# A residual block stack on one Trainium2 core: the modulation's scaling and sums moved between the two pairs of units of a feed-forward quad

## The chip, the cores and the metric

One core of one Trainium2 chip runs the whole program. The metric is device time of one execution in microseconds (us); the median of three runs is given.

## The reference

A first block of two layers works on 16 meta tokens and 256 tokens of width 1024: a feed-forward, a mixer (a short convolution, then differential attention), a second feed-forward, each with an RMS norm before and behind it. That makes four feed-forwards, numbered 0 to 3 here. A second block of two layers follows, whose norms are scaled, shifted and gated by a modulation computed from a vector c:

```
def swiglu(h, w_gu, w_down):
    g, u = jnp.split(h @ w_gu, 2, axis=-1)
    return (jax.nn.silu(g) * u) @ w_down
...
cond = jax.nn.silu(c)
for l in range(DEPTH):
    mod = cond @ ada_w[l] + ada_b[l]
    shift, scale, gate = jnp.split(mod, 3, axis=-1)
    h = rms_norm_2(x, norm_g[l]) * (1.0 + scale[:, None, :]) + shift[:, None, :]
```

The hidden width of a feed-forward is 2816, and `ada_w` has 1024 x 3072 numbers for each of two layers. The modulation depends on c alone, so it can be computed at any time before the second block.

## The kernel before

**Units and quads.** All large weights come in units of 128 output columns, four units a quad, one for each of four slots of the buffers `raw`, `w_hi` and `w_lo`. A unit (i, s) goes through: SyncE loads `raw` slot s (L543); ScalarE rounds it to `w_hi` (`split_hi`, L591) once the slot's earlier unit is through on TensorE; VectorE makes `w_lo = raw - w_hi` (`split_lo`, L1069); TensorE multiplies three times for each of 8 chunks of 128 rows (L1773 to L1775), since each operand is split in an upper and a lower half.

**A feed-forward** (`ffn(k)`, stages `gu{k}` and `dn{k}`) has two halves. The first has 11 quads (0 to 10). The units of a quad are gate, up, gate, up: two pairs p = 0, 1, each giving one of 22 hidden chunks. Per pair VectorE scales the gate's bank (`tg`, L1167) and the up's bank (`ur`, L1170), multiplies (`full`, L1175) behind ScalarE's SiLU (`silu`, L679), ScalarE rounds the product to `a_hi` (`hi`, L683), VectorE subtracts to `a_lo` (`lo`, L1181). In quad i both engines also split the units of quad i+1. The second half, the down projection, has 4 quads of wider units (1408 columns of a slot, 33 matmuls); units 0 and 1 of a quad fill bank 0 with hidden chunks 0 to 10 and 11 to 21, units 2 and 3 bank 2. Feed-forwards 0 to 2 work on 272 tokens, feed-forward 3 on 256.

**The modulation** is computed in the shadow: 12 pieces per feed-forward (`ada_w`, 512 KB each). SyncE loads a piece into the one buffer `ada_raw` (L554), ScalarE scales its eight parts by `cond` (`am`, L667), VectorE adds them up in three steps (`a0`, `a1`, `ar`; L1157, L1160, L1163).

**What orders the work.** Each engine runs its instructions in the order written. An engine counts its steps on a semaphore of its own, in the order that `vec.phase` and `act.phase` declare (L297, L298), and others wait for a count. SyncE's queue repeats: the four weight loads of quad i (slot s waits for `w_lo` of unit (i-1, s)), then the modulation piece i, which waits for `ar` of quad i-1:

```
def load_ada(k, i):
...
    sp.wait_ge(vec.sem, gu_step(vec, f"gu{k}", "ar", i - 1))
...
with sp.Fori(2 if stage[:2] == "gu" else 1, n) as i:
    load(stage, i)
    if stage[:2] == "gu":
        load_ada(k, i)
```

The functions that the diff touches, with what calls them:

Of the kernel before, what the change touches and what calls it, by code (L numbers as in the profile page):

```python
# [117 lines left out]
def build(nc, w8, w11, ada_w, params_in, consts_in, masks_in, pool_w, bands_in, fl_w, x_in, out):  # L118
    ctx = ExitStack()
    with ctx:  # L120
# [110 lines left out]
        act, vec, pe, pool = (Steps(sem(n)) for n in ("scalar_steps", "vector_steps", "tensor_steps", "gpsimd_steps"))  # L231
# [56 lines left out]
        def declare_ffn(k):  # L288
            g, d = f"gu{k}", f"dn{k}"
            if k == 0:  # L290
                act.phase("pre0", [f"hi{c}" for c in range(DC)] + [f"sq{c}" for c in range(DC)])
                vec.phase("pre0", [f"lo{c}" for c in range(DC)])
            act.phase(g + "q", ["am"])
            declare_stat(f"pre{k}")
            act.phase(g + "r", ["silu0", "silu1", "hi0", "hi1"])
            vec.phase(g + "q", ["a0", "a1", "ar", "tg0", "ur0", "tg1", "ur1", "full0", "lo0", "full1", "lo1"])
            act.phase(g, ["am", "silu0", "hi0", "silu1", "hi1"], 10)  # L297
            vec.phase(g, ["tg0", "a0", "a1", "ar", "ur0", "full0", "lo0", "tg1", "ur1", "full1", "lo1"], 10)  # L298
            act.phase(d + "a", ["am"])
            act.phase(d, ["sq0", "f0", "sq1", "f1"], 4)  # L300
            pool.phase(d, ["zero"])
            pool.phase(d + "s", ["add0", "add1"], 3)
            pool.phase(d + "t", ["add0"])
            vec.phase(d, ["a0", "a1", "ar"])
            declare_res(f"res{k}")
            pe.phase(d, ["ada"])
# [276 lines left out]
        def _(sc):  # L583
# [79 lines left out]
            def ada(phase, i):  # L663

                sc.wait_ge(ada_in, 16 * i + 16)
                for c in range(DC):
                    last = sc.activation(ada_raw[:, c, :], ada_raw[:, c, :], ACT.Copy, scale=cond[:, c:c + 1])  # L667
                last.then_inc(act.step(phase, "am"), 1)

            def ffn(k):  # L670
                g, d = f"gu{k}", f"dn{k}"
                n = width(g)
                ada(g + "q", 12 * k)
                token_norm(f"pre{k}")
                sc.preload_act_table(ACT.Silu)

                def silu(phase, p, i):
                    sc.wait_ge(vec.sem, gu_step(vec, g, f"tg{p}", i))
                    sc.activation(silu_t[:, p, 0:n], xt[:, p, 0:n], ACT.Silu).then_inc(act.step(phase, f"silu{p}"), 1)  # L679

                def upper_a(phase, p, i):
                    sc.wait_ge(vec.sem, gu_step(vec, g, f"full{p}", i))
                    sc.activation(a_hi[:, bass.ds(2 * i + p, 1), 0:n].rearrange("p a t -> p (a t)"), u_t[:, p, 0:n], ACT.Copy  # L683
                                  ).then_inc(act.step(phase, f"hi{p}"), 1)

                for p in range(2):
                    silu(g + "r", p, 0)
                for p in range(2):
                    upper_a(g + "r", p, 0)

                def gu_quad(i):
                    ada(g, 12 * k + i)
                    for p in range(2):
                        split_next(g, i, 2 * p)
                        silu(g, p, i)
                        split_next(g, i, 2 * p + 1)
                        upper_a(g, p, i)

                gu_quad(1)
                with sc.Fori(2, 10) as i:  # L700
                    gu_quad(i)
                gu_quad(10)

                sc.preload_act_table_set("natural_log_exp_and_others")
                ada(d + "a", 12 * k + 11)
                first = GAIN[f"res{k}"][1]

                def dn_quad(i):
                    q = FIRST_QUAD[d] + i
                    for p in range(2):  # L710
                        o = 2 * i + p
                        split_next(d, i, 2 * p)
                        sc.wait_ge(unit_done, SLOTS * q + 2 * p + 2)
                        if not isinstance(i, int) or i > 0:
                            sc.wait_ge(pool.sem, pool.at(d + "s", f"add{p}", i - 1))
                        sc.activation(sq[:, p, 0:n], bank[2 * p][:, 0:n], ACT.Square).then_inc(act.step(d, f"sq{p}"), 1)  # L716
                        sc.activation(f[:, bass.ds(o, 1), 0:n].rearrange("p a t -> p (a t)"), bank[2 * p][:, 0:n],
                                      ACT.Copy, scale=half_g[:, first, bass.ds(o, 1)]).then_inc(act.step(d, f"f{p}"), 1)
                        if not (isinstance(i, int) and i == 3 and p == 1):
                            split_next(d, i, 2 * p + 1)  # L720

                quads(d, dn_quad)
                res_norm(f"res{k}")
# [339 lines left out]
        def _(ve):  # L1063
# [86 lines left out]
            def ffn(k):  # L1150
# [27 lines left out]
                def lower_a(phase, p, i):  # L1178
                    at = bass.ds(2 * i + p, 1)
                    ve.wait_ge(act.sem, gu_step(act, g, f"hi{p}", i))  # L1180
                    ve.tensor_tensor(a_lo[:, at, 0:n].rearrange("p a t -> p (a t)"), u_t[:, p, 0:n],  # L1181
                                     a_hi[:, at, 0:n].rearrange("p a t -> p (a t)").bitcast(F32), ALU.subtract
                                     ).then_inc(vec.step(phase, f"lo{p}"), 1)
# [14 lines left out]
                def gu_quad(i):  # L1198
                    q = FIRST_QUAD[g] + i
                    for p in range(2):  # L1200
                        ve.wait_ge(unit_done, SLOTS * q + 2 * p + 1)
                        gate(g, p, bank[2 * p])
                        split_next(g, i, 2 * p)
                        if p == 0:
                            ada(g, i, i - 1, act.at(g, "am", i - 1))
                        ve.wait_ge(unit_done, SLOTS * q + 2 * p + 2)
                        ve.wait_ge(vec.sem, gu_step(vec, g, f"lo{p}", i - 1))
                        up(g, p, bank[2 * p + 1])
                        full(g, p, i)
                        split_next(g, i, 2 * p + 1)  # L1210
                        lower_a(g, p, i)

                gu_quad(1)
                with ve.Fori(2, 10) as i:
# [554 lines left out]
        def _(te):  # L1769
# [119 lines left out]
            def ada(k, units):  # L1889

                for i in units:
                    last = te.matmul(ADA[:, i:i + 1], ada_sum[:, i, :], ones[:, 0:1], start=True, stop=True)
                return last
# [11 lines left out]
            def ffn(k):  # L1905
                g, d = f"gu{k}", f"dn{k}"
                n = width(g)
                free = lambda s, i: (vec.sem, gu_step(vec, g, ("tg", "ur")[s % 2] + str(s // 2), i))
                second_quad(f"pre{k}", g, n, free(3, 0))
                later_quads(g, n, free)  # L1910

                def dn_quad(i):
                    q = FIRST_QUAD[d] + i
                    for s in range(SLOTS):
                        te.wait_ge(w_lo_ready, SLOTS * q + s + 1)
                        p = s // 2
                        if isinstance(i, int) and i == 0:
                            if s == 0:
                                te.wait_ge(vec.sem, vec.at(g, "lo0", 9))
                            if s == 1:  # L1920
                                te.wait_ge(vec.sem, vec.at(g, "lo1", 9))
                        elif s % 2 == 0:
                            te.wait_ge(act.sem, act.at(d, f"f{p}", i - 1))
                        if isinstance(i, int) and i == 3 and s == 3:
                            res_most(f"res{k}", pool.at(d + "t", "add0"))
                        for kk in range(HALF):
                            kc = HALF * (s % 2) + kk
                            last = product(bank[2 * p][:, 0:n], s, kk, a_hi[:, kc, 0:n], a_lo[:, kc, 0:n],
                                           kc == 0, kc == FC - 1)
                        last.then_inc(unit_done, 1)  # L1930
                dn_quad(0)
                with te.Fori(1, 3) as i:
                    dn_quad(i)
                dn_quad(3)
                te.wait_ge(vec.sem, vec.at(d, "ar"))
                ada(k, range(2))
                res_last(f"res{k}", act.at(d, "sq1", 3))
                ada(k, range(2, 12)).then_inc(pe.step(d, "ada"), 1)
# [576 lines left out]
```

## Time and profile before

| | |
|---|---|
| median of 3 runs | 1402.84 us (1402.38 to 1402.99) |
| profiled execution | 1399.22 us, its span 1397.4 us |
| TensorE busy | 1334.0 us (95%) |
| VectorE busy | 920.1 us (66%) |
| ScalarE busy | 806.8 us (58%) |
| GpSimd busy | 81.0 us (6%) |
| DMA | 239.99 MB, mean 172 GB/s |

Times in the trace are from the start of the span. A row of a timeline gives an instruction's start, its length, engine, line and operands, and in brackets how long the engine stood idle before it and what ended that. PE is TensorE, DVE VectorE, ACT ScalarE, SP SyncE. Lengths of pipelined instructions overlap a little with the next; what an instruction takes of its engine is the distance between two starts.

### The profile page before, as it was taken

The page shows a single profiled execution, that of the slowest core. Times are in us where ns is not written, and L with a number is a line of the kernel's source. Part 1 is how long each engine was busy: PE and PEld are TensorE (multiplying, and loading weights), DVE is VectorE, ACT ScalarE, POOL GpSimd, SP SyncE. Part 2 cuts the span into 40 slices and gives each one's busy share as a digit, 9 for nine tenths or more (in the row PEclk, how much of TensorE's full clock was granted, in tenths as well). Part 3 has the DMA queues.
Part 4 walks back from the last instruction along what each step waited for, and adds up shares of the span by engine and source line. Part 5 has one row for each costly group of instructions (what it writes and reads, how often), then busy time and mean ns, then how long its engine had stood idle before and what let it go on. Part 6 is the DMA issues. An engine that isn't in the chain of part 4 may idle for free.

```text
span 1397.4 us, 27554 instructions
## 1 busy us (share of the span) xinstructions
PE 1334.0 (95%) x10214; PEld 1288.2 (92%) x10214; DVE 920.1 (66%) x1525; ACT 806.8 (58%) x1570; POOL 81.0 (6%) x81
## 2 busy tenths in 40 slices
PE   6999999998999999999999999899999899989997
PEld 6999999998999999999998988799999899977787
DVE  5777536866777536777536776577764574666774
ACT  6666544446666546666535555676664543457663
POOL 2000011012000001000001000300000000010000
PEclk9999999999999999999999999999999999999999
DMA  5766653653766652766643441466675254445441
GB/s 192 248 225 237 228 186 123 187 166 107 247 224 240 227 168 87 246 228 236 225 140 109 128 122 48 136 227 226 225 248 163 71 181 121 132 136 147 121 125 35
DMA packets 63314, 239.99 MB, mean 172 GB/s; under 512 B 7024, under 2 KB 8448, under 8 KB 63104
## 3 DMA queue, kind: packets, MB, share of 16 engines
q1 hardware_dynamic: 63168, 238.84, 51.9%
q8 instruction: 56, 0.92, 0.3%
q14 instruction: 26, 0.21, 0.0%
q0 software_dynamic: 64, 0.02, 0.0%
HBM read 237.76 MB, written 1.05 MB: 171 GB/s over the span
## 4 chain that ended last, share of the span: by engine, by line
PE 75%; DVE 10%; ACT 8%; issue 4%; DMA 2%; DVEq 0%; ACTq 0%; POOL 0%; SPq 0%; POOLq 0%
PE bank L1773 20%; PE bank L1775 20%; PE bank L1774 19%; DVE w_lo L1069 4%; PE bank L1780 3%; ACT w_hi L591 2%; ACT ada_raw L667 2%; PE bank L1845 2%; PE bank L1846 1%; PE bank L1838 1%; PE bank L1781 1%; PE bank L2154 1%; DVE ada_raw L1157 1%; DMA ada_raw<-ada_w 1%; DMA raw<-w 1%
## 5 line engine op out<-in xcount | busy, mean ns | idle before, releaser
L1069 DVE TENSOR_TENSOR w_lo<-raw,w_hi 128x1024 fp32r<-128x1024 f32 (+2 forms) x376 | 489.8, 1306 | 321.1 <-ACT w_hi L591 320.6
L1773 PE MATMUL bank<-x_hl,w_hi 128*128 128x272 f32 (+1 forms) x1776 | 516.5, 291 | 15.0 <-DVE w_lo L1069 14.7
L1775 PE MATMUL bank<-x_hl,w_lo 128*128 128x272 f32 (+1 forms) x1776 | 511.0, 288 | 0.0
L1774 PE MATMUL bank<-x_hl,w_hi 128*128 128x272 f32 (+1 forms) x1776 | 509.3, 287 | 0.0
L591 ACT ACTIVATE w_hi<-raw 128x1024 fp32r<-128x1024 f32 (+2 forms) x376 | 411.9, 1101 | 125.7 <-PE bank L1775 107.1
L1773 PEld LDWEIGHTS bank<-x_hl,w_hi 128*128 128x128 f32 x1776 | 335.7, 189 | 18.0 <-ACT arena L627 8.7
L1774 PEld LDWEIGHTS bank<-x_hl,w_hi 128*128 128x128 f32 x1776 | 338.4, 191 | 0.6
L1775 PEld LDWEIGHTS bank<-x_hl,w_lo 128*128 128x128 f32 x1776 | 335.4, 189 | 0.0
L1773 PE MATMUL bank<-a_hi,w_hi 128*128 128x272 f32 (+1 forms) x960 | 279.1, 291 | 11.7 <-DVE w_lo L1069 3.4
L1775 PE MATMUL bank<-a_hi,w_lo 128*128 128x272 f32 (+1 forms) x960 | 275.1, 287 | 0.0
L1774 PE MATMUL bank<-a_lo,w_hi 128*128 128x272 f32 (+1 forms) x960 | 274.6, 286 | 0.0
L1773 PEld LDWEIGHTS bank<-a_hi,w_hi 128*128 128x128 f32 x960 | 182.4, 190 | 14.6 <-DVE w_lo L1069 7.2
L1774 PEld LDWEIGHTS bank<-a_lo,w_hi 128*128 128x128 f32 x960 | 182.7, 190 | 0.4
L1775 PEld LDWEIGHTS bank<-a_hi,w_lo 128*128 128x128 f32 x960 | 182.1, 190 | 0.0
L667 ACT ACTIVATE ada_raw<-ada_raw,cond 128x128 f32<-128x128 f32 x384 | 117.5, 389 | 0.9 <-DMA ada_raw<-ada_w 0.8
L683 ACT ACTIVATE a_hi<-arena 128x272 f32 (+3 forms) x88 | 37.7, 429 | 125.6 <-DVE arena L1175 125.2
L1780 PE MATMUL bank<-x_hl,w_hi 128*128 128x512 f32 x256 | 92.2, 400 | 4.4 <-DVE x_hl L1107 2.8
L1781 PE MATMUL bank<-x_hl,w_lo 128*128 128x256 f32 x256 | 71.7, 280 | 0.0
L1780 PEld LDWEIGHTS bank<-x_hl,w_hi 128*128 128x128 f32 x256 | 48.1, 188 | 16.0 <-issue 5.0
L716 ACT ACTIVATE sq<-bank 128x272 f32<-128x272 f32 (+1 forms) x32 | 12.6, 394 | 85.9 <-PE bank L1775 85.9
L1717 POOL TENSOR_TENSOR sq_sum<-sq_sum,sq 128x272 f32<-128x272 f32 (+1 forms) x28 | 21.4, 764 | 702.3 <-ACT sq L716 702.3
L1845 PE MATMUL bank<-x_hl,w_hi 128*128 128x272 f32 (+1 forms) x144 | 43.0, 321 | 10.4 <-ACT x_hl L623 8.2
(275 smaller groups left out, 1423.1 us busy)
## 6 DMA issues: line engine op xcount, KB each, us to landing
raw<-w SPq DMA_DIRECT2D x312, 512.0 KB, 4.4
raw<-w SPq DMA_DIRECT2D x64, 704.0 KB, 4.6
ada_raw<-ada_w SPq DMA_DIRECT2D x48, 512.0 KB, 3.6
h<-x_in SPq DMA_DIRECT2D x1, 1088.0 KB, 5.3
work<-bands SPq DMA_DIRECT2D x1, 544.0 KB, 7.0
cst<-consts SPq DMA_DIRECT2D x1, 528.0 KB, 4.6
out<-h SPq DMA_DIRECT2D x1, 512.0 KB, 3.0
out<-h SPq DMA_DIRECT2D x4, 128.0 KB, 2.3
```

Of the source, the lines that this page charges most:

```text
L591: sc.activation(w_hi[:, s, a:n], raw[:, s, a:n], ACT.Copy).then_inc(w_hi_ready, 1)
L667: last = sc.activation(ada_raw[:, c, :], ada_raw[:, c, :], ACT.Copy, scale=cond[:, c:c + 1])
L683: sc.activation(a_hi[:, bass.ds(2 * i + p, 1), 0:n].rearrange("p a t -> p (a t)"), u_t[:, p, 0:n], ACT.Copy).then_inc(act.step(phase, f"hi ...
L1069: ve.tensor_tensor(w_lo[:, s, a:n], raw[:, s, a:n], w_hi[:, s, a:n].bitcast(F32), ALU.subtract).then_inc(w_lo_ready, 1)
L1157: ve.tensor_tensor(ada_raw[:, 0:4, :], ada_raw[:, 0:4, :], ada_raw[:, 4:8, :], ALU.add).then_inc(vec.step(phase, "a0"), 1)
L1717: gp.tensor_tensor(sq_sum[:, 0:n], sq_sum[:, 0:n], sq[:, p, 0:n], ALU.add).then_inc(pool.step(phase, f"add{p}"), 1)
L1773: te.matmul(dst, w_hi[:, s, a:a + P], rhs_hi, start=first, stop=False)
L1774: te.matmul(dst, w_hi[:, s, a:a + P], rhs_lo, start=False, stop=False)
L1775: return te.matmul(dst, w_lo[:, s, a:a + P], rhs_hi, start=False, stop=last)
L1780: te.matmul(dst.rearrange("p (a t) -> p a t", a=2), w_hi[:, s, a:a + P], both, start=first, stop=False)
L1781: return te.matmul(dst[:, 0:SEQ], w_lo[:, s, a:a + P], both[:, 0, :], start=False, stop=last)
L1845: te.matmul(dsts[s][:, 0:n], w_hi[:, s, k * P:(k + 1) * P], x_hi[:, k, 0:n], start=k == 0, stop=False)
```

## The change

In quads 1 to 10 of each feed-forward's first half the scaling of a modulation piece (`ada` on ScalarE) stood ahead of the quad's first split, and its sums (`ada` on VectorE) between the first split and `ur0`. Both now stand behind the first pair: behind `hi0` on ScalarE, behind `lo0` on VectorE. The declared orders are changed to match. In the second half, the first unit waited for `lo0` of quad 10; it now waits for `tg0` of quad 10, which is the step that reads bank 0 last; the hidden chunks 0 to 10 that it reads are made in quads 0 to 5.

```diff
--- before.py
+++ after.py
@@ -294,8 +294,8 @@
             declare_stat(f"pre{k}")
             act.phase(g + "r", ["silu0", "silu1", "hi0", "hi1"])
             vec.phase(g + "q", ["a0", "a1", "ar", "tg0", "ur0", "tg1", "ur1", "full0", "lo0", "full1", "lo1"])
-            act.phase(g, ["am", "silu0", "hi0", "silu1", "hi1"], 10)
-            vec.phase(g, ["tg0", "a0", "a1", "ar", "ur0", "full0", "lo0", "tg1", "ur1", "full1", "lo1"], 10)
+            act.phase(g, ["silu0", "hi0", "am", "silu1", "hi1"], 10)
+            vec.phase(g, ["tg0", "ur0", "full0", "lo0", "a0", "a1", "ar", "tg1", "ur1", "full1", "lo1"], 10)
             act.phase(d + "a", ["am"])
             act.phase(d, ["sq0", "f0", "sq1", "f1"], 4)
             pool.phase(d, ["zero"])
@@ -689,12 +689,13 @@
                     upper_a(g + "r", p, 0)
 
                 def gu_quad(i):
-                    ada(g, 12 * k + i)
                     for p in range(2):
                         split_next(g, i, 2 * p)
                         silu(g, p, i)
                         split_next(g, i, 2 * p + 1)
                         upper_a(g, p, i)
+                        if p == 0:
+                            ada(g, 12 * k + i)
 
                 gu_quad(1)
                 with sc.Fori(2, 10) as i:
@@ -1201,14 +1202,14 @@
                         ve.wait_ge(unit_done, SLOTS * q + 2 * p + 1)
                         gate(g, p, bank[2 * p])
                         split_next(g, i, 2 * p)
-                        if p == 0:
-                            ada(g, i, i - 1, act.at(g, "am", i - 1))
                         ve.wait_ge(unit_done, SLOTS * q + 2 * p + 2)
                         ve.wait_ge(vec.sem, gu_step(vec, g, f"lo{p}", i - 1))
                         up(g, p, bank[2 * p + 1])
                         full(g, p, i)
                         split_next(g, i, 2 * p + 1)
                         lower_a(g, p, i)
+                        if p == 0:
+                            ada(g, i, i - 1, act.at(g, "am", i - 1))
 
                 gu_quad(1)
                 with ve.Fori(2, 10) as i:
@@ -1916,7 +1917,7 @@
                         p = s // 2
                         if isinstance(i, int) and i == 0:
                             if s == 0:
-                                te.wait_ge(vec.sem, vec.at(g, "lo0", 9))
+                                te.wait_ge(vec.sem, vec.at(g, "tg0", 9))
                             if s == 1:
                                 te.wait_ge(vec.sem, vec.at(g, "lo1", 9))
                         elif s % 2 == 0:
```

ScalarE, the loop over quads 2 to 9 of feed-forward 0, before (`ada_raw` scaled, `raw_in0` to `raw_in2` the weight slots):

```order
L667 ACTIVATE ada_raw<-ada_raw,cond 128x128 [waits ada_in]
L667 ACTIVATE ada_raw<-ada_raw,cond 128x128 x7
L590 ISA [waits raw_in0]
L591 ACTIVATE w_hi<-raw 128x1024 [waits unit_done]
L679 ACTIVATE silu_t<-xt 128x272 [waits vector_steps]
L590 REGISTER_ALU [waits raw_in1]
L591 ACTIVATE w_hi<-raw 128x1024 [waits unit_done]
L683 ISA [waits vector_steps]
L683 ACTIVATE a_hi<-arena 128x272
L590 REGISTER_ALU [waits raw_in2]
L591 ACTIVATE w_hi<-raw 128x1024 [waits unit_done]
```

and in the changed kernel, where the file's lines behind the edit are one further:

```order
L590 ISA [waits raw_in0]
L591 ACTIVATE w_hi<-raw 128x1024 [waits unit_done]
L679 ACTIVATE silu_t<-xt 128x272 [waits vector_steps]
L590 REGISTER_ALU [waits raw_in1]
L591 ACTIVATE w_hi<-raw 128x1024 [waits unit_done]
L683 ISA [waits vector_steps]
L683 ACTIVATE a_hi<-arena 128x272
L667 ACTIVATE ada_raw<-ada_raw,cond 128x128 [waits ada_in]
L667 ACTIVATE ada_raw<-ada_raw,cond 128x128 x7
L590 REGISTER_ALU [waits raw_in2]
L591 ACTIVATE w_hi<-raw 128x1024 [waits unit_done]
```

The eight scalings have moved from the quad's start to the place between `a_hi` of the first pair and `w_hi` of slot 2.

VectorE, the same loop before (`xt<-bank0` is `tg0`, `arena<-bank1` is `ur0`, `arena<-arena,silu_t` is `full0`, `a_lo` is `lo0`, `xt<-bank2` is `tg1`):

```order
L1167 TENSOR_TENSOR xt<-bank0,arena 128x272 [waits unit_done]
L1069 TENSOR_TENSOR w_lo<-raw,w_hi 128x1024 [waits w_hi_ready]
L1157 TENSOR_TENSOR ada_raw<-ada_raw 128x512 [waits scalar_steps]
L1160 TENSOR_TENSOR ada_raw<-ada_raw 128x256 [waits vector_steps]
L1163 TENSOR_TENSOR arena<-ada_raw 128x128
L1207 ISA [waits unit_done]
L1170 TENSOR_TENSOR arena<-bank1,arena 128x272 [waits vector_steps]
L1175 TENSOR_TENSOR arena<-arena,silu_t 128x272 [waits scalar_steps]
L1069 TENSOR_TENSOR w_lo<-raw,w_hi 128x1024 [waits w_hi_ready]
L1181 TENSOR_TENSOR a_lo<-arena,a_hi 128x272
L1167 TENSOR_TENSOR xt<-bank2,arena 128x272 [waits unit_done]
L1069 TENSOR_TENSOR w_lo<-raw,w_hi 128x1024 [waits w_hi_ready]
```

and in the changed kernel:

```order
L1168 TENSOR_TENSOR xt<-bank0,arena 128x272 [waits unit_done]
L1070 TENSOR_TENSOR w_lo<-raw,w_hi 128x1024 [waits w_hi_ready]
L1171 TENSOR_TENSOR arena<-bank1,arena 128x272 [waits vector_steps]
L1176 TENSOR_TENSOR arena<-arena,silu_t 128x272 [waits scalar_steps]
L1070 TENSOR_TENSOR w_lo<-raw,w_hi 128x1024 [waits w_hi_ready]
L1182 TENSOR_TENSOR a_lo<-arena,a_hi 128x272
L1158 TENSOR_TENSOR ada_raw<-ada_raw 128x512 [waits scalar_steps]
L1161 TENSOR_TENSOR ada_raw<-ada_raw 128x256 [waits vector_steps]
L1164 TENSOR_TENSOR arena<-ada_raw 128x128
L1168 TENSOR_TENSOR xt<-bank2,arena 128x272 [waits unit_done]
L1070 TENSOR_TENSOR w_lo<-raw,w_hi 128x1024 [waits w_hi_ready]
```

The three additions on `ada_raw` and its sum have moved from ahead of the wait for the second unit to behind `a_lo` of the first pair; so has the step `ar`, for which SyncE's next modulation load waits.

## Rows read from the trace of the kernel before

**Rows 1.** The page, part 1: busy us (share) xinstructions.

```profile
PE 1334.0 (95%) x10214; PEld 1288.2 (92%) x10214; DVE 920.1 (66%) x1525; ACT 806.8 (58%) x1570; POOL 81.0 (6%) x81
```

**Rows 2.** Timeline of TensorE, feed-forward 0: start us, us, line, [idle before <-releaser].

```profile
40.10 0.39 PE L1773 MATMUL bank<-x_hl,w_hi 128*128 128x272 f32 x1 [1.12 <-DVE w_lo L1069]
...
43.45 0.39 PE L1773 MATMUL bank<-x_hl,w_hi 128*128 128x272 f32 x1
...
149.01 0.29 PE L1773 MATMUL bank<-a_hi,w_hi 128*128 128x272 f32 x1
```

**Rows 3.** Windows: us, busy of each engine (x), granted clock, DMA share, GB/s.

```profile
52.78:64.26 11.48, 11.48 (x93) 11.48 (x93) 8.96 (x16) 7.77 (x16) 0.00 (x0) 1.00 0.67 230
956.14:967.52 11.38, 11.38 (x99) 11.38 (x98) 8.83 (x16) 7.74 (x16) 0.00 (x0) 1.00 0.65 230
1027.60:1033.50 5.90, 5.86 (x27) 5.89 (x28) 4.39 (x6) 4.97 (x10) 0.00 (x0) 0.50 0.97 369
```

**Rows 4.** Timeline of VectorE, one quad of feed-forward 0.

```profile
84.30 1.23 DVE L1069 TENSOR_TENSOR w_lo<-raw,w_hi 128x1024 fp32r<-128x1024 f32 x1 [2.06 <-ACT w_hi L591]
85.44 0.68 DVE L1157 TENSOR_TENSOR ada_raw<-ada_raw 128x512 f32<-128x512 f32 x1
...
86.75 0.29 DVE L1163 TENSOR_TENSOR arena<-ada_raw 128x128 f32 x1 [0.17 <-DVE ada_raw L1160]
86.97 0.44 DVE L1170 TENSOR_TENSOR arena<-bank,arena 128x272 f32<-128x272 f32 x1
87.54 0.44 DVE L1175 TENSOR_TENSOR arena<-arena,silu_t 128x272 f32<-128x272 f32 x1
87.90 1.22 DVE L1069 TENSOR_TENSOR w_lo<-raw,w_hi 128x1024 fp32r<-128x1024 f32 x1
```

**Rows 5.** Timeline of ScalarE, the same quad.

```profile
80.53 0.43 ACT L683 ACTIVATE a_hi<-arena 128x272 f32 x1 [0.77 <-DVE arena L1175]
80.87 2.45 ACT L667 ACTIVATE ada_raw<-ada_raw,cond 128x128 f32<-128x128 f32 x8
83.22 1.04 ACT L591 ACTIVATE w_hi<-raw 128x1024 fp32r<-128x1024 f32 x1
...
88.12 0.43 ACT L683 ACTIVATE a_hi<-arena 128x272 f32 x1 [2.59 <-DVE arena L1175]
```

**Rows 6.** Timeline of SyncE's queue, that quad, then feed-forward 3.

```profile
87.21 0.33 SPq L554 DMA_DIRECT2D ada_raw<-ada_w  x1
88.09 0.33 SPq L543 DMA_DIRECT2D raw<-w  x1
...
912.54 0.33 SPq L554 DMA_DIRECT2D ada_raw<-ada_w  x1
```

**Rows 7.** DMA, us to landing: 40 to 140; then issued 88.1; 934.3; 913.2.

```profile
raw<-w SPq DMA_DIRECT2D x32, 512.0 KB, 4.7
ada_raw<-ada_w SPq DMA_DIRECT2D x9, 512.0 KB, 3.5
...
raw<-w SPq DMA_DIRECT2D x1, 512.0 KB, 3.9
...
raw<-w SPq DMA_DIRECT2D x1, 512.0 KB, 5.4
...
raw<-w SPq DMA_DIRECT2D x1, 512.0 KB, 4.2
```

**Rows 8.** Timeline of TensorE, feed-forward 3's two waits.

```profile
920.80 0.47 PE L1773 MATMUL bank<-x_hl,w_hi 128*128 128x256 f32 x1 [2.38 <-DVE w_lo L1069]
...
1027.64 0.55 PE L1773 MATMUL bank<-a_hi,w_hi 128*128 128x256 f32 x1 [2.82 <-DVE a_lo L1181]
```

**Rows 9.** Timeline of ScalarE, feed-forward 3, quad 1.

```profile
918.45 1.04 ACT L591 ACTIVATE w_hi<-raw 128x1024 fp32r<-128x1024 f32 x1
```

**Rows 10.** Timeline of VectorE, feed-forward 0, quad 10.

```profile
142.48 1.63 DVE L1069 TENSOR_TENSOR w_lo<-raw,w_hi 128x1408 fp32r<-128x1408 f32 x1 [1.86 <-ACT w_hi L591]
...
152.38 0.43 DVE L1181 TENSOR_TENSOR a_lo<-arena,a_hi 128x272 fp32r<-128x272 f32 x1
```

## The prediction

> **What bounds the kernel now.** I read the busy shares first: TensorE is busy 95% of the span and VectorE 66% [rows 1], so time can come or go only where TensorE waits or slows. In the feed-forwards a unit of 24 matmuls takes (149.01 - 43.45) / 35 = 3.016 us, a quad of four 12.06 us [rows 2]. Then I looked at what keeps pace with it. The windows between two issues of a modulation load are 11.48 us long with 272 tokens, and 11.38 us with 256 [rows 3]: that is one turn of a ring between ScalarE and VectorE, and it is shorter than TensorE's quad. So this ring has 0.58 us in hand per quad in feed-forwards 0 to 2. In feed-forward 3 the quad has 256 columns for 272, so 12.06 x 256 / 272 = 11.35 us on TensorE; the ring has nothing in hand, and TensorE waits at both ends: 2.38 us at quad 2, 2.82 us at the first unit of the second half [rows 8].
>
> The reader should follow one quad on three engines. VectorE waits 2.06 us for ScalarE's w_hi, then makes w_lo, then the three additions, then ur0, full0 and the next w_lo [rows 4]. ScalarE does the eight scalings right behind hi1, and w_hi behind them [rows 5]. SyncE issues the next modulation load 0.17 us after the last addition ends (86.75 + 0.29 to 87.21), and the next quad's first weights 0.88 us behind it [rows 6]. That second issue is what matters: the weights of unit (i+2, 0) stand in SyncE's queue behind the modulation load i+1, and this one waits for the sums of quad i ("ar").
>
> **The change, part by part.** It removes no instruction and adds none: eight scalings and three additions a quad are moved, and one wait names an earlier step.
>
> The move on ScalarE: w_hi of slot 0 no longer stands behind the scalings. At quad 2 of feed-forward 3 w_hi began at 918.45, although its weights, issued at 913.2, had landed at 917.4 [rows 7, 9]: 1.0 us is saved there. For feed-forwards 0 to 2, where the wait is 1.12 us in all [rows 2], I take 0.5 us each, between nothing (weights land last) and 1.1 us.
>
> The move on VectorE: "ar" now ends behind w_lo of slot 1 and lo0. What is queued behind it on SyncE is the modulation load, and the weights of slots 0 and 1 of the quad after next. They closed no ring that mattered before: "ar", landing, w_hi, w_lo, additions was 0.17 + 5.6 + 0.04 + 1.08 + 1.14 + 1.60 = 9.6 us. Now the whole first pair lies in this ring. One turn, each piece from start to start:
> - end of "ar" to the modulation load's issue: 0.17 [rows 6]
> - from there until the weights of slot 0 land: 0.88 + 4.7 = 5.6 (the median landing) [rows 6, 7]
> - to the start of w_hi 0.04 (my estimate), w_hi to w_lo (83.22 to 84.30) 1.08 [rows 4, 5]
> - w_lo to ur0 1.14, as w_lo to the first addition now; ur0 to full0 0.57 [rows 4]
> - full0 to hi0 (87.54 to 88.12) 0.58; hi0 to the scalings, as hi1 to them now, 0.34 [rows 4, 5]
> - the eight scalings 2.45 and 0.05 to VectorE [rows 5]
> - first addition to the end of "ar", 1.60 [rows 4]
>
> The sum is 13.6 us. ScalarE's w_hi of slot 1 fits into it as long as its weights land no more than 2.3 us after those of slot 0. The bounds: the earliest landing found is 0.88 + 3.9 = 4.8 us, the latest 0.88 + 5.4 = 6.3 us after the modulation load [rows 7], which gives 12.8 to 14.3. The new order issues slots 0 and 1 close together behind the modulation load, as at the stage's entry in feed-forward 3, where it was 0.7 + 4.2 = 4.9 us (912.54 to 913.2, and the landing) [rows 6, 7]. So I take 5.5, a little under the median: **13.5 us a turn**. It is longer than TensorE's 12.06 and 11.35, and TensorE has no lead (it waits at quad 2 before). From there on it goes at the ring's pace.
>
> In numbers, feed-forward 0: unit (2,0) starts at 39.6 (40.10 less 0.5). Nine turns later, plus 0.75 for the wider split of the down projection (1.63 for 1.23 [rows 4, 10], and about as much on ScalarE), its first unit starts at 39.6 + 121.5 + 0.75 = 161.9, where it was 149.01 [rows 2]. The mended wait (tg0 instead of lo0) can't help there: w_lo of that very unit is what is late. The second unit still needs lo1. From the start of the first wide w_lo to the end of lo1 (152.38 + 0.43) VectorE has 10.3 us of work without a wait [rows 10]; in the new order it also waits some 1.2 us for the scalings. So lo1 ends 11.5 us after that w_lo's start (160.2), at 171.7, and TensorE, through with its first unit at 166.0, **waits almost 6 us**; before, the second unit started at 153.2. Shift: 18.6 us. Behind so long a wait the clock drops: the 2.82 us wait in feed-forward 3 was followed by 5.9 us at 0.50, that is 1.2 GHz, which cost half of it, 2.9 us [rows 3, 8]. 21.5 us for each of feed-forwards 0 to 2, 64.5 in all.
>
> Feed-forward 3: 919.8 + 121.5 + 0.75 = 1042.1 for the first unit, second at +9.9 = 1052.0. Before it was 1027.64 + 33 x 0.118 + 2.9 = 1034.4 for the second, the clock's loss included. 17.6 + 2.9 for the new wait = 20.5. Afterwards the down projection is TensorE's own pace as before: nothing is given back.
>
> Sum: 64.5 + 20.5 = **85 us**. The profiled execution took 1399.22 us (span 1397.4), the median is 1402.84; I add it to the median: 1488.
>
> On landing times the Trainium skill (DMA: Bandwidth & Descriptors, "Anatomy of one DMA") has 2.0 us fixed and bytes / 436 GB/s per transfer, for GpSimd's path. For 512 KB that is 3.2 us; the trace has 3.5 for a modulation load that flies alone. For the weights right behind it that rule gives about 4.4 us from the modulation load's issue, where rows say 5.6: the trace's are slower, and I go by it. By the rule's the turn would be 12.4 us and the sum some 45 us.
>
> **The rivals.**
> - The ring stays hidden, and the kernel gets faster. This needs a turn under 12.06 us, so a landing within 4.0 us of the modulation load's issue. For it speaks only that the pieces overlap in ways I may have missed; against it that none of the landings looked at is under 4.8 [rows 7]. Gain: entries 1.5 + 1.0, the 2.82 us wait and its 2.9 us of clock, 8.2 us: 1395.
> - A shorter ring: the weights land as a load alone in flight does, 0.88 + 3.5 = 4.4 us after the modulation load's issue [rows 6, 7], and the turn is 12.4. Each 0.1 us of the turn is 9 x 4 x 0.1 = 3.6 us, so 85 - 40 = 45: 1448. For it speaks the 4.9 us at the entry; against it the median.
> - The clock. TensorE's slack of 1.4 us per quad shows as two short waits (slot 0 for its weights, slot 2 because its w_lo now stands behind the additions). If each quad ran 5.9 us at half clock, TensorE would need 12.06 + 2.9 = 15.0 us for it, 1.5 over the ring: 36 x 1.5 = 54 more, 1542. Against it: after the 1.12 us wait at 40.10, the unit still took 3.35 us to 43.45, 0.33 over a full one, so no stretch of half clock followed [rows 2]. The Trainium skill (TensorE: Matmul & The Clock Gate, "A second HAM failure mode: psum-queue depth-cycling") tells of a kernel whose clock swung because of frequent short idles; this trace has no such place in the feed-forwards, so it stays a small chance.
> - The new wait changes nothing. This is part of the forecast for the first unit: the relaxed wait is overtaken by w_lo.
>
> **How the numbers follow.** The forecast, a turn of 13.0 to 14.2 us, has 0.78; the short ring 0.09; the clock 0.06; hidden and faster 0.05; anything near no change 0.02. The time is 1488. Range: the turn's ends alone give 85 - 25 (12.8) to 85 + 29 (14.3), 1463 to 1517; the clock's term may be 0 to 5.8 instead of 2.9 a stage, and the turn could sit nearer the short ring, so I take 1450 to 1515. 0.2% is about what a measurement of this kernel can tell from no change. Faster 0.05, same 0.01, slower 0.94.
>
> **What would show it.** In the changed profile modulation loads should be issued 13.5 us apart (11.48 before), both token counts alike; VectorE should wait for w_hi of slot 0 by the weights' landing, not by the scalings; TensorE should wait up to 1 us twice a quad for w_lo, and some 6 us for lo1 at each down projection's second unit, with a granted clock of 0.5 after it. The 2.82 us wait for lo0 should be gone by name only. The prediction is wrong if the loads stay at or under 12.06 us apart, which means the weights land within 4 us, or if SyncE doesn't hold the weights behind "ar".

## The result and the profile after

The changed kernel takes 1506.91 us (median of 6 runs, 1499.24 to 1510.86), the kernel before 1402.61 us in the same comparison (6 runs). The ratio is 1.0736, its 95% interval 1.0708 to 1.0764: slower by 104 us, inside the range and 19 us over the forecast. The page of the changed kernel, first its span, the busy shares, the granted clock by slices and the shares of the chain that ended last:

```profile
span 1507.4 us, 27554 instructions
...
PE 1361.3 (90%) x10214; PEld 1300.2 (86%) x10214; DVE 923.2 (61%) x1525; ACT 810.0 (54%) x1570; POOL 83.0 (6%) x81
...
PEclk9999999999999999999999999999999999999998
...
PE 52%; ACT 13%; DVE 13%; DMA 12%; issue 7%; SPq 1%; DVEq 1%; ACTq 0%; POOL 0%; POOLq 0%
```

TensorE was busy 95% before [rows 1] and is busy 90% of a longer span now. DMA holds 12% of the chain, on the page of before 2%. The granted clock reads 9 tenths in every slice but the last, so its drops are short ones. Who waited for whom, from the view of the waits, the changed kernel's two rows first and the same two of before behind them:

```profile
engine line waited for: us in total, times, longest us
...
ACT w_hi L591 <- DMA raw<-w: 147.8, 57, 4.3
...
PE bank L1774 <- DVE w_lo L1070: 82.6, 77, 8.4
...
PE bank L1773 <- DVE w_lo L1069: 18.1, 11, 8.6
...
ACT w_hi L591 <- DMA raw<-w: 4.3, 3, 2.0
```

TensorE waits 82.6 us for w_lo in 77 waits, most of them one or two a quad, where it waited 18.1 us in 11; behind that stands ScalarE waiting for weights, 147.8 us in 57 waits, before 4.3 us in 3. One turn of the ring in feed-forward 0, on SyncE's queue:

```profile
116.12 0.33 SPq L554 DMA_DIRECT2D ada_raw<-ada_w  x1
117.00 2.99 SPq L543 DMA_DIRECT2D raw<-w  x4
130.93 0.33 SPq L554 DMA_DIRECT2D ada_raw<-ada_w  x1
```

The distance of the two modulation loads is 130.93 - 116.12 = 14.81 us, where it was 11.48 [rows 3]; the ten loads from 43.50 to 173.30 us have a mean distance of 14.42 us. The same nine turns of feed-forwards 1, 2 and 3 have means of 14.46, 14.28 and 14.18 us, so all 36 have 14.34. The weights behind the load at 116.12, and the medians of a longer stretch (KB each, us to landing):

```profile
raw<-w SPq DMA_DIRECT2D x1, 512.0 KB, 5.8
...
raw<-w SPq DMA_DIRECT2D x28, 512.0 KB, 6.6
ada_raw<-ada_w SPq DMA_DIRECT2D x7, 512.0 KB, 3.6
```

All four weight loads of the quad were issued in one burst behind the modulation load (the merged row at 117.00 is four of them within 2.99 us). The first lands after 5.8 us, that is 6.7 us behind the modulation load; before, the median was 4.7 us from its own issue, 5.6 in all [rows 6, 7]. The turn shown is one of the slower ones, and the medians are over all four slots. Over the 36 turns the first weight load behind a modulation load landed 5.4 us after its own issue on average and 6.2 us after the modulation load's; in the same places before it was 4.8 and 5.7. ScalarE stands there when they land:

```profile
122.95 1.06 ACT L591 ACTIVATE w_hi<-raw 128x1024 fp32r<-128x1024 f32 x1 [4.03 <-DMA raw<-w]
...
126.33 0.43 ACT L683 ACTIVATE a_hi<-arena 128x272 f32 x1 [1.06 <-DVE arena L1176]
126.67 2.44 ACT L667 ACTIVATE ada_raw<-ada_raw,cond 128x128 f32<-128x128 f32 x8
```

and VectorE takes it on (w_lo, ur0, full0, then the sums):

```profile
124.04 1.23 DVE L1070 TENSOR_TENSOR w_lo<-raw,w_hi 128x1024 fp32r<-128x1024 f32 x1 [3.86 <-ACT w_hi L591]
125.19 0.43 DVE L1171 TENSOR_TENSOR arena<-bank,arena 128x272 f32<-128x272 f32 x1
125.76 0.44 DVE L1176 TENSOR_TENSOR arena<-arena,silu_t 128x272 f32<-128x272 f32 x1
...
129.15 0.69 DVE L1158 TENSOR_TENSOR ada_raw<-ada_raw 128x512 f32<-128x512 f32 x1 [1.46 <-ACT ada_raw L667]
...
130.46 0.29 DVE L1164 TENSOR_TENSOR arena<-ada_raw 128x128 f32 x1 [0.17 <-DVE ada_raw L1161]
```

Read as a ring: landed at 122.8, w_hi 122.95, w_lo 124.04, ur0 125.19, full0 125.76, hi0 126.33, the scalings 126.67, the first addition 129.15, end of the sums 130.75, next load 130.93. Every piece but the landing has, within 0.1 us, the length that was read from the trace of before [rows 4, 5]. The window of this turn and the one behind the wait for lo1 (us, busy of PE, PEld, DVE, ACT, POOL, granted clock, DMA share, GB/s):

```profile
116.12:130.93 14.81, 12.55 (x98) 12.12 (x98) 9.03 (x16) 7.87 (x16) 0.00 (x0) 1.00 0.48 177
178.00:184.00 6.00, 5.99 (x32) 6.00 (x33) 1.63 (x1) 3.47 (x9) 0.00 (x0) 0.64 0.90 354
```

and the waits of TensorE: the two of that turn, then at the down projection of feed-forward 0 (first and second unit) and of feed-forward 3 (second unit):

```profile
117.57 0.38 PE L1774 MATMUL bank<-x_hl,w_hi 128*128 128x272 f32 x1 [0.70 <-DVE w_lo L1070]
...
125.41 0.39 PE L1774 MATMUL bank<-x_hl,w_hi 128*128 128x272 f32 x1 [1.56 <-DVE w_lo L1070]
...
168.19 0.39 PE L1774 MATMUL bank<-a_hi,w_hi 128*128 128x272 f32 x1 [1.26 <-DVE w_lo L1070]
...
178.01 0.57 PE L1774 MATMUL bank<-a_hi,w_hi 128*128 128x272 f32 x1 [5.42 <-DVE a_lo L1182]
...
1138.00 0.55 PE L1774 MATMUL bank<-a_hi,w_hi 128*128 128x256 f32 x1 [5.58 <-DVE a_lo L1182]
```

In this turn TensorE stays at full clock despite its waits of 0.70 and 1.56 us. The first unit waits for its own w_lo, not for lo0, and the second 5.42 us for lo1 (5.58 in feed-forward 3). The second units of the four feed-forwards start at 178.01, 519.35, 753.31 and 1138.00 us; the same matmuls of before at 153.1, 467.2, 675.1 and 1034.3 (each the 33rd behind the first unit's start). The shifts are 24.9, 52.1, 78.3 and 103.7 us: about 26 us in each feed-forward.

The spans of the two profiled executions differ by 110.0 us, more than the medians. Of the 6.3 us behind that last point, 1.6 is the low clock right behind the second unit, and 2.7 and 2.0 us come in the second block, where this trace has these stretches of low clock:

```profile
1202.90:1216.50 13.60, 10.85 (x36) 8.63 (x37) 10.50 (x21) 6.47 (x16) 0.00 (x0) 0.63 0.13 39
1475.90:1493.00 17.10, 14.38 (x97) 12.54 (x91) 5.51 (x17) 6.08 (x16) 0.00 (x0) 0.80 0.01 1
```

At the first of these the trace of before has one short stretch of low clock (0.81 over 9 us from 1095), at the second none. They are not the ring's: e1 below, whose ring is open, has the first too (0.63), and e4, on the kernel before, the second (0.80).

### The profile page after: what moved, and what is told of

The parts are those of the page before. It is cut to its first block, busy times and chain, and to the rows that moved or that the text cites. A ratio compares the mean times of both kernels' runs of the same rounds, so it can differ in the third digit from the quotient of the medians.

```text
span 1507.4 us, 27554 instructions
## 1 busy us (share of the span) xinstructions
PE 1361.3 (90%) x10214; PEld 1300.2 (86%) x10214; DVE 923.2 (61%) x1525; ACT 810.0 (54%) x1570; POOL 83.0 (6%) x81
## 4 chain that ended last, share of the span: by engine, by line
PE 52%; ACT 13%; DVE 13%; DMA 12%; issue 7%; SPq 1%; DVEq 1%; ACTq 0%; POOL 0%; POOLq 0%
PE bank L1774 12%; PE bank L1776 12%; PE bank L1775 12%; DMA raw<-w 12%; ACT ada_raw L667 6%; DVE w_lo L1070 3%; ACT w_hi L591 3%; PE bank L1781 2%; DVE ada_raw L1158 2%; PE bank L1846 1%; PE bank L1839 1%; DVE arena L1176 1%; PE bank L1847 1%; DVE ada_raw L1161 1%; DVE arena L1171 1%
## 5 line engine op out<-in xcount | busy, mean ns | idle before, releaser
L1774 PE MATMUL bank<-x_hl,w_hi 128*128 128x272 f32 (+1 forms) x1776 | 522.1, 294 | 75.3 <-DVE w_lo L1070 75.2
L591 ACT ACTIVATE w_hi<-raw 128x1024 fp32r<-128x1024 f32 (+2 forms) x376 | 412.3, 1102 | 261.6 <-DMA raw<-w 147.8
L1775 PE MATMUL bank<-x_hl,w_hi 128*128 128x272 f32 (+1 forms) x1776 | 508.9, 287 | 0.0
L1774 PE MATMUL bank<-a_hi,w_hi 128*128 128x272 f32 (+1 forms) x960 | 282.8, 295 | 34.8 <-DVE a_lo L1182 21.8
L1774 PEld LDWEIGHTS bank<-a_hi,w_hi 128*128 128x128 f32 x960 | 185.6, 193 | 39.3 <-DVE w_lo L1070 31.7
L1775 PEld LDWEIGHTS bank<-a_lo,w_hi 128*128 128x128 f32 x960 | 185.9, 194 | 0.3
L1158 DVE TENSOR_TENSOR ada_raw<-ada_raw 128x512 f32<-128x512 f32 x48 | 33.2, 691 | 56.1 <-ACT ada_raw L667 56.1
```

The lines of the kernel that those rows point to most:

```text
L591: sc.activation(w_hi[:, s, a:n], raw[:, s, a:n], ACT.Copy).then_inc(w_hi_ready, 1)
L1158: ve.tensor_tensor(ada_raw[:, 0:4, :], ada_raw[:, 0:4, :], ada_raw[:, 4:8, :], ALU.add).then_inc(vec.step(phase, "a0"), 1)
L1774: te.matmul(dst, w_hi[:, s, a:a + P], rhs_hi, start=first, stop=False)
L1775: te.matmul(dst, w_hi[:, s, a:a + P], rhs_lo, start=False, stop=False)
```

## The experiments

Theory A: the loss is a ring through SyncE's queue. The weights of the next quad stand behind the modulation load, this waits for the sums, and the sums now stand behind the first pair. The rivals: B, the later place of the scalings and sums costs by itself on ScalarE and VectorE; C, landings don't depend on what flies beside them; D, the relaxed wait of the first unit is worth something; E and F are told at their runs. The times below are compared with runs of the kernel before on the same chip: 1400.19 us for the first four, 1402.00 us for the last three.

**e1, the weights of slots 0 and 1 ahead of the modulation load.**

```diff
-                with sp.Fori(2 if stage[:2] == "gu" else 1, n) as i:
-                    load(stage, i)
-                    if stage[:2] == "gu":
-                        load_ada(k, i)
+                    with sp.Fori(2, n - 1) as i:
+                        load(stage, i, (2, 3))
+                        load(stage, i + 1, (0, 1))
+                        load_ada(k, i)
```

(and the same at the stage's first and last quads; every load waits for what it waited for.)

> The changed kernel with SyncE's queue reordered: the weight loads of slots 0 and 1 of the next quad go ahead of the modulation load that waits for the quad's sums. ScalarE, VectorE and TensorE are as in the changed kernel. Theory A (the ring runs through SyncE: weights held behind the modulation load, which waits for the sums): the ring is cut, modulation loads come as often as TensorE's quads, 12.06 us apart with 272 tokens and about 11.4 with 256, and the whole kernel takes 1388 to 1400 us, below the kernel before. Theory B (the later place of the scalings and sums on ScalarE and VectorE costs by itself, in w_lo of slot 2 above all): 1470 us or more, loads still over 13.5 us apart.

Measured: 1390.55 us, ratio 0.9928 (0.9911 to 0.9944). The kernel is faster than both: the order of SyncE's queue is worth (1.0736 - 0.9928) x 1402 = 113 us on the changed engines. Its modulation loads, from the timeline of SyncE's queue:

```profile
86.99 0.33 SPq L554 DMA_DIRECT2D ada_raw<-ada_w  x1
...
99.04 0.33 SPq L554 DMA_DIRECT2D ada_raw<-ada_w  x1
```

are 12.05 us apart, TensorE's own pace; the three turns ahead of them took 10.8 to 10.9 us. What is left of TensorE's waits in feed-forward 3, at slot 2 of quad 2 and at the second unit of the down projection:

```profile
920.57 0.39 PE L1788 MATMUL bank<-x_hl,w_hi 128*128 128x256 f32 x1 [0.52 <-DVE w_lo L1084]
...
1022.02 0.36 PE L1788 MATMUL bank<-a_hi,w_hi 128*128 128x256 f32 x1 [0.75 <-DVE a_lo L1196]
```

stands against 2.38 and 2.82 us before [rows 8], each with a clock of 0.50 behind it (3.1 us from 921.10, and [rows 3]). Theory A holds, B falls: ScalarE, VectorE and TensorE run the changed order here.

**e2, the scalings back at the quad's start**, the sums left behind lo0.

```diff
                 def gu_quad(i):
+                    ada(g, 12 * k + i)
                     for p in range(2):
...
-                        if p == 0:
-                            ada(g, 12 * k + i)
```

> The changed kernel with ScalarE's eight scalings back at the quad's start; VectorE's sums stay behind lo0. Theory A: the ring still holds SyncE's queue, but goes from full0 by w_lo of slot 1 and lo0 to the sums (0.36 + 1.14 + 0.35 us) in place of hi0 and the scalings (0.58 + 0.34 + 2.5): 1.6 us shorter, turns of about 13.0 us for 14.4, 36 x 1.5 = 54 us less than the changed kernel: about 1453 us (1435 to 1470). Theory B (the place of the scalings is what costs, as they hold w_hi of slot 2): back to 1410 us or less.

Measured: 1456.72 us, ratio 1.0406 (1.0389 to 1.0423). The turn, from SyncE's queue:

```profile
94.25 0.33 SPq L554 DMA_DIRECT2D ada_raw<-ada_w  x1
...
107.25 0.33 SPq L554 DMA_DIRECT2D ada_raw<-ada_w  x1
```

is 13.00 us; the nine of feed-forward 0 have a mean of 12.82, 1.60 less than 14.42. The ring is shorter by what was taken out of it, as A worked out to 4 us, and is still there.

**e3, modulation loads of half the size.** Half of each piece but a feed-forward's first is not read, and ScalarE's eight scalings read the half that is there, so the modulation is not the reference's.

```diff
-                sp.dma_start(ada_raw[:, :, :], ada_w[bass.ds(12 * k + i, 1), :, :, :]...
+                m = DC if isinstance(i, int) and i == 0 else DC // 2
+                sp.dma_start(ada_raw[:, 0:m, :], ada_w[bass.ds(12 * k + i, 1), :, 0:m, :]...
```

> The changed kernel with modulation loads of half the size (256 KB for 512; the other half of each piece is not read, ScalarE still makes eight scalings and VectorE the same sums, of the half that is there). Theory A with the landing set by what flies together (the burst moves some 320 to 400 GB/s): the weights behind it land 0.6 to 0.8 us earlier, turns of 13.7 us for 14.4, about 1482 us (1472 to 1490). Theory C (the landing is a fixed time after each issue, whatever flies beside it): no change, 1500 us or more.

Measured: 1467.24 us, ratio 1.0476 (1.0458 to 1.0493), 15 us below what A said, under its range of 1472 to 1490, and far from C. The weights behind the load at 98.0, then the medians of a longer stretch:

```profile
raw<-w SPq DMA_DIRECT2D x1, 512.0 KB, 3.9
...
raw<-w SPq DMA_DIRECT2D x31, 512.0 KB, 5.2
ada_raw<-ada_w SPq DMA_DIRECT2D x8, 256.0 KB, 2.6
```

The first weights land in 3.9 us (5.8 in the changed kernel at the same place in the turn). Ten modulation loads from 44.68 to 162.73 us are 13.12 us apart on average, 1.3 us less than 14.42. Taking 256 KB out of the burst gave more than its bytes at the burst's rate (0.8 us): the direction is shown, the size of it I had too small, and no run says why. Over all 36 turns it is the landing that gained it: the first weights landed 1.1 us earlier behind the modulation load's issue (5.1 for 6.2), and the turn was 1.1 us shorter (13.22 for 14.34).

**e4, the relaxed wait alone**, on the kernel before.

```diff
-                                te.wait_ge(vec.sem, vec.at(g, "lo0", 9))
+                                te.wait_ge(vec.sem, vec.at(g, "tg0", 9))
```

> The kernel before with the third part of the change alone: the down projection's first unit waits for tg0 of quad 10, not lo0. Theory A: the first unit of feed-forward 3 starts almost 3 us earlier, but the second then waits for lo1 some 5 us in place of none: nothing gained, 1400 to 1405 us. Rival D (the relaxed wait is worth its 2.82 us and the clock behind it): 1395 to 1399 us.

Measured: 1402.23 us, ratio 1.0015 (1.0004 to 1.0026): no gain. The second unit of feed-forward 3's down projection, from the timeline of TensorE:

```profile
1032.57 0.36 PE L1773 MATMUL bank<-a_hi,w_hi 128*128 128x256 f32 x1 [3.69 <-DVE a_lo L1181]
```

waits 3.69 us for lo1, where A had some 5. The wait has moved one unit on: TensorE is 3.9 us ahead of the kernel before in the first unit and 0.1 us ahead once the second unit's low clock is over.

**e5, e1's queue on the engines of the kernel before.**

> The kernel before with SyncE's queue reordered as in e1 (weights of slots 0 and 1 of the next quad ahead of the modulation load), all engines otherwise as before. Theory A (what counts is which work shares SyncE's one queue with which wait): in the old order the scalings stand at the quad's start, and now their load is issued only behind w_lo of slot 1 of the quad before; the ring then goes from w_lo of slot 1 by the load's issue and landing (3.6 us), the scalings, w_hi and w_lo of slot 0, the sums, ur0, full0 to the next w_lo of slot 1: longer than 12.06 us, loads about 13.6 us apart, some 1480 us (1450 to 1510). Theory E (the reordered queue is a gain by itself, whatever the engines' order): 1400 us or less.

Measured: 1482.89 us, ratio 1.0588 (1.0555 to 1.0621). The same edit that takes 113 us from the changed kernel adds 81 us to the kernel before. SyncE's queue (a weight load, then the modulation loads):

```profile
82.95 0.33 SPq L543 DMA_DIRECT2D raw<-w  x1
83.57 0.33 SPq L554 DMA_DIRECT2D ada_raw<-ada_w  x1
...
96.85 0.33 SPq L554 DMA_DIRECT2D ada_raw<-ada_w  x1
```

The turn is 13.28 us, the mean in feed-forward 0 13.75. Here ScalarE, with the scalings at the quad's start, waits for the modulation load itself:

```profile
101.61 2.46 ACT L681 ACTIVATE ada_raw<-ada_raw,cond 128x128 f32<-128x128 f32 x8 [2.23 <-DMA ada_raw<-ada_w]
```

2.23 us idle, and w_hi of slot 0 stands behind the scalings. E falls: neither order is good by itself; the two must fit.

**e6, the hold kept, the weights first behind it.** As e1, with one line more ahead of the two weight loads, `sp.wait_ge(vec.sem, gu_step(vec, f"gu{k}", "ar", i - 1))`.

> The changed kernel with the hold kept but the order behind it turned: SyncE waits for the sums of the quad before, as in the changed kernel, then issues the weights of slots 0 and 1, then the modulation load. Theory A: the ring is still there, but the weights start 0.9 us earlier and ahead of the modulation's 512 KB, so they land in 3.5 to 4.7 us from the issue in place of 6.7 from the end of the hold; turns of 12.1 to 12.7 us, 1400 to 1445 us. Rival F (the hold costs nothing by itself, only the modulation load's bytes ahead of the weights do): as e1, 1388 to 1395 us.

Measured: 1411.32 us, ratio 1.0068 (1.0045 to 1.0092). From SyncE's queue:

```profile
78.97 0.33 SPq L557 DMA_DIRECT2D ada_raw<-ada_w  x1
79.84 10.84 SPq L543 DMA_DIRECT2D raw<-w  x4
90.87 0.33 SPq L557 DMA_DIRECT2D ada_raw<-ada_w  x1
```

The turn is 11.90 us, a little under A's 12.1 to 12.7, so inside the quads of 272 tokens TensorE's 12.06 us rules again; with 256 it is too long for 11.35 us. At each down projection's second unit TensorE still waits for lo1, longest in feed-forward 3:

```profile
1040.24 0.55 PE L1795 MATMUL bank<-a_hi,w_hi 128*128 128x256 f32 x1 [5.56 <-DVE a_lo L1203]
```

In feed-forwards 0 to 2 that wait is 2.37, 3.90 and 3.47 us. Against e1 the second units with the clock behind them lose 2.1, 5.2, 4.7 and 7.6 us, 19.6 in all, about what e6 is slower by. Why lo1 comes so late there, no run separates.

The medians of its loads (weights, modulation piece):

```profile
raw<-w SPq DMA_DIRECT2D x32, 512.0 KB, 5.2
ada_raw<-ada_w SPq DMA_DIRECT2D x9, 512.0 KB, 5.7
```

The modulation load, now third in the burst, lands in 5.7 us, where it took 3.6 as the first. The first weights land 3.7 us after their own issue (the load at 77.86), where it was 5.8, and are issued 0.9 us sooner. So the 113 us between the changed kernel and e1 have two parts: (1.0736 - 1.0068) x 1402 = 94 us go when the weights are issued ahead of the modulation load, 20 us more when the hold goes. F falls, the hold has a price of its own.

**e7, e1 with the wait for lo0 again.**

> e1 with the third part of the change undone: the down projection's first unit waits for lo0 of quad 10 again. Theory A: with the ring cut VectorE is in time with lo0, the second unit's wait for lo1 sets the time either way, and the time is that of e1, 1388 to 1393 us. Rival D: the relaxed wait carries a part of e1's gain, 1394 us or more.

Measured: 1389.60 us, ratio 0.9907 (0.9883 to 0.9931), the same as e1. The third part of the change is worth nothing on the kernel before (e4) or with the ring open (e7). With the ring closed it was not run alone, but there the first unit waits for its own w_lo (1.26 us at 168.19), which the relaxed wait can't move. D falls.

## Why the prediction was right, and which term was off

**The mechanism** was right in its steps. The ring closed through SyncE's queue (e1 opens it, and the loss is gone); ScalarE waits for the landing, not for the scalings; loads of both token counts come equally far apart (14.42 us in feed-forward 0, and (1133.35 - 1005.69) / 9 = 14.18 us in feed-forward 3, issue to issue); TensorE waits twice a quad, 0.70 and 1.56 us where up to 1 us was forecast; and the down projection's second unit waits for lo1, 5.42 us for the 6 forecast. The steps between landing and sums were sized right: 130.93 - 122.8 = 8.1 us, against 8.0 in the sum.

**The mis-sized term** is "from there until the weights of slot 0 land". I took 5.5 us, the median less a little, because the first loads of a stage had landed early. It measured 6.7 us in the turn shown and 6.2 us on average over all 36 turns. The reason that I gave for going under the median, that slots 0 and 1 would be issued close together, speaks the other way: the hold gathers all four weight loads and the modulation load into one burst of 2.5 MB, and the median landing of a weight load rose from 4.7 [rows 7] to 6.6 us. e3 shows that the bytes of the burst ahead of a weight load set a part of it. That the loads close behind it set another is read from the two traces alone: the modulation load ahead is the same in both, and the first weights took 4.8 us before and 5.4 after.

The turn was 14.34 us on average where I had 13.5: 36 x 0.84 = 30 us more. That is over the band of 13.0 to 14.2 us to which the 0.78 was given, and over my upper bound of 14.3, taken from the latest landing seen; single turns took up to 14.9. By my own sum it gives 1488 + 30 = 1518 us, outside the range of 1450 to 1515; the time fell inside it by luck, because smaller terms took 11 us back.

One reading was wrong as well. The 3.5 us of a modulation load was not that of a load alone in flight, since a weight load goes out 0.88 us behind it [rows 6]; with four close behind it, it still took 3.6. The Trainium skill's figures for one transfer (DMA: Bandwidth & Descriptors, "Anatomy of one DMA": 2.0 us and bytes at 436 GB/s, on GpSimd's path) lead further away: the prediction's estimate by them was 4.4 us from the modulation load's issue, and here five loads are in flight and it was 6.2.

**What took part of it back.** The shift of the second unit in feed-forward 0 was 24.9 us, 6.3 more than the 18.6 forecast, not 8: the ring's first load went out at 43.50 us, and the prediction's start (w_lo of unit (2,0) at 38.3, the sums 6.7 us later) puts it at 45.2. The clock behind the wait for lo1 cost less than 2.9 us in feed-forward 0: 6 us at a mean of 0.64 lose 2.2 us, because the clock had already fallen inside the wait.

**The relaxed wait** did nothing, as said, and e4 adds that it does nothing on the kernel before either.

**The rivals**: the hidden ring needed a landing within 4.0 us of the modulation load's issue, and none came under 5.2; the short ring took 4.4 us, which only e3's half loads come near (4.7 at the least); the clock did not swing with the short waits (1.00 in the turn's window, with 2.2 us of TensorE's idle in it). It did fall in one of the 36 turns, in feed-forward 3 behind the longest of these waits, and 3.2 us at 0.50 followed; so this rival was small, not empty (the wait, then the window's clock):

```profile
1086.31 0.38 PE L1774 MATMUL bank<-x_hl,w_hi 128*128 128x256 f32 x1 [2.12 <-DVE w_lo L1070]
...
1086.90:1090.10 3.20, 3.20 (x17) 3.20 (x16) 1.75 (x4) 2.91 (x10) 0.00 (x0) 0.50 0.01 3
```

**The gain that the change could have had** is e1's: the changed engines' order with SyncE's queue fitted to it, 1390.55 us.

## What to carry to other kernels

A queue that is served in order hands on every wait in it to what stands behind. Before moving the step for which a load waits, list what is queued behind that load, and follow the turn round: step, issue, landing, use, step. If its length is over the bounding engine's own pace, it sets the pace, whatever else looks hidden. Size the landing from the traffic that the new order makes, not from the old trace's median: here a hold that releases five loads at once left the first of them as fast as before (3.6 us, before 3.5) and made the four behind it late (median 6.6 us for 4.7). And an order of loads and an order of work are one decision: each of the two here was a loss alone (104 us and 81 us), both together a gain of 10.

## What the runs showed of the hardware

- A load's landing time depends on the loads around it, on those ahead above all. The first weight load behind a modulation load of 512 KB took 5.8 us and behind one of 256 KB 3.9; a modulation load took 3.6 us as the first of a burst and 5.7 us as the third. Loads close behind matter less: none for the modulation load (3.5 before, 3.6 with four loads close behind it), some 0.6 us for the first weights (4.8 to 5.4 on average), and no run varies these alone.
- The cost of low clock behind a long wait isn't in proportion to the wait. After 5.42 us of waiting TensorE's matmuls ran 4.3 us at 0.50 (from 178.01), after 5.58 us 3.4 us (from 1138.00), after 2.82 us 5.9 us [rows 3, 8], and after 5.56 us in e6 6 us. In each of these the clock fell inside the wait, and only what was left of the low stretch when the work came back cost time. In e4, after 3.69 us, it fell 0.7 us behind the wait (0.59 over 1032.57 to 1036.60). The windows are of the changed kernel, the last of e6:

```profile
175.60:178.00 2.40, 0.00 (x0) 0.02 (x1) 2.27 (x3) 1.95 (x3) 0.00 (x0) 0.50 1.03 387
178.01:182.20 4.19, 4.18 (x18) 4.19 (x19) 0.69 (x1) 3.46 (x9) 0.00 (x0) 0.50 0.97 375
182.40:188.40 6.00, 6.00 (x50) 6.00 (x49) 2.36 (x2) 2.05 (x3) 0.78 (x1) 1.00 0.59 203
1138.00:1141.30 3.30, 3.30 (x15) 3.30 (x16) 0.00 (x0) 3.30 (x9) 0.00 (x0) 0.50 0.98 384
...
1040.20:1046.20 6.00, 5.96 (x28) 5.99 (x29) 0.00 (x0) 3.45 (x9) 0.00 (x0) 0.50 0.88 364
```
